# Order of 32 experts in a weight-streaming mixture-of-experts stage: number order with single blocks last, against heavy and light in turn

## The reference, cut to what matters

```
logits = x @ w_router + b_router
top_logit, top_idx = lax.top_k(logits, 4); gate = softmax(top_logit)
per expert e, over its tokens:
    h = x @ w_up[e] + b_up[e]              # 1024 -> 2048
    glu, lin = split(h); glu = min(glu, 7); lin = clip(lin, -7, 7)
    y = (glu * sigmoid(1.702 * glu) * (lin + 1)) @ w_down[e] + b_down[e]
    out[token] += gate * y
```

## Time and profile before

| | |
|---|---|
| runs shown | 1345.87 us median (1345.58 to 1346.92) |
| profiled execution, its time | 1348.95 us |
| profiled execution, its span | 1347.1 us |
| TensorE matmul busy | 1146.1 us, 85% of the span |
| DMA | 463.78 MB, mean 344 GB/s over the span |
| weight pieces | 192 of 2048 KB, 128 of `w_up` and 64 of `w_down` |
| mean granted TensorE clock | 0.93 of full speed |

### The profile page before, as it was taken

The page is one execution under the profiler, slowest core; times in us unless marked ns, Lnnn a source line. Parts: engine busy times, 40 slices in busy tenths (PEclk is TensorE's granted clock), DMA queues, the critical chain, the costliest instruction groups (busy, mean ns, idle before and its releaser), DMA issues.

```text
span 1347.1 us, 28518 instructions
## 1 busy us (share of the span) xinstructions
PE 1146.1 (85%) x10974; PEld 532.9 (40%) x10975; DVE 489.4 (36%) x1218; ACT 200.1 (15%) x297; POOL 224.7 (17%) x392
## 2 busy tenths in 40 slices
PE   6999999976999999999997987989889789964540
PEld 3445554543444444444543433424334334421120
DVE  2273453453334333333432332323333233321117
ACT  2114321011111111111211111111111111110001
POOL 1000012001222222222221211212122112210003
PEclk9999999986999999999998999989899889987775
DMA  9303005449699999979999999999999999999987
GB/s 341 117 1 125 16 1 221 154 175 406 268 421 414 415 417 423 426 293 426 426 427 426 426 424 427 426 427 424 424 425 419 423 428 425 426 427 426 424 328 302
DMA packets 51088, 463.78 MB, mean 344 GB/s; under 512 B 9052, under 2 KB 10264, under 8 KB 25976
## 3 DMA queue, kind: packets, MB, share of 16 engines
q1 hardware_dynamic: 41184, 441.89, 78.8%
q0 software_dynamic: 7632, 20.85, 4.0%
q10 hardware_dynamic: 2248, 0.71, 0.2%
HBM read 446.65 MB, written 16.78 MB: 344 GB/s over the span
## 4 chain that ended last, share of the span: by engine, by line
DMA 44%; PE 44%; SPq 4%; DVE 4%; issue 3%; ACT 0%; POOL 0%; ACTq 0%; POOLq 0%; DVEq 0%
DMA W<-in_w_up_dram 41%; PE B L1361 17%; PE B L1140 12%; PE B L1376 8%; PE B L1261 4%; SPq L305 1%; SPq L310 1%; DMA W<-yrow 1%; SPq L385 1%; SPq L387 1%; DMA yrow<-misc,idx_s 1%; DMA misc<-hsrow,idx_g 1%; DVE W L1112 0%; PE B L1284 0%; DMA W<-in_b_spatial_dram 0%
## 5 line engine op out<-in xcount | busy, mean ns | idle before, releaser
L1361 PE MATMUL B<-W,misc 128*32 128x512 f32 x4992 | 596.6, 626 | 124.4 <-DMA W<-in_w_up_dram 95.4
L1361 PEld LDWEIGHTS B<-W,misc 128*32 128x32 f32 x4992 | 188.1, 113 | 484.1 <-issue 474.8
L1376 PE MATMUL B<-W,misc 128*32 128x256 f32 x4992 | 289.0, 382 | 0.9 <-DVE misc L1053 0.9
L1376 PEld LDWEIGHTS B<-W,misc 128*32 128x32 f32 x4992 | 192.7, 111 | 120.3 <-issue 52.3
L1036 DVE TENSOR_TENSOR misc<-B,misc 128x512 f32<-128x512 f32 x78 | 54.0, 692 | 418.2 <-PE B L1361 418.2
L1140 PE MATMUL B<-W 128*128 128x512 f32 x384 | 171.2, 601 | 0.0
L671 ACT ACTIVATE misc<-misc 128x256 f32<-128x256 f32 x78 | 32.5, 416 | 850.4 <-DVE misc L1038 850.4
L502 POOL COPY idx_g<-idx_tab 128x1 uint32 (+1 forms) x79 | 15.0, 190 | 594.0 <-DVE misc L1067 576.7
L1140 PEld LDWEIGHTS B<-W 128*128 128x128 f32 x384 | 72.8, 194 | 85.6 <-issue 85.6
L514 POOL DMA_INDIRECT yrow<-misc,idx_s x78 | 78.4, 1006 | 160.0 <-DVE misc L1055 160.0
L671 ACT ACT_TABLE_LOAD x78 | 100.1, 1283 | 4.9 <-DVE idx_tab L1013 3.5
(11 more groups left out here) (257 smaller groups left out, 484.9 us busy)
## 6 DMA issues: line engine op xcount, KB each, us to landing
W<-in_w_up_dram SPq DMA_DIRECT2D x128, 2048.0 KB, 10.6
W<-in_w_down_dram SPq DMA_DIRECT2D x64, 2048.0 KB, 10.0
W<-in_w_in_dram SPq DMA_DIRECT2D x6, 2048.0 KB, 18.1
W<-yrow SPq DMA_DIRECT2D x4, 2048.0 KB, 14.5
W<-in_x_dram SPq DMA_DIRECT2D x8, 512.0 KB, 5.4
W<-in_w_out_dram SPq DMA_DIRECT2D x1, 4096.0 KB, 12.9
hres<-W SPq DMA_DIRECT2D x4, 512.0 KB, 2.6
hsrow<-W SPq DMA_DIRECT2D x4, 512.0 KB, 3.6
```

Source lines behind the costliest of these rows:

```text
L1361: ins = mm(B[0][BT * j:BT * (j + 1), :].rearrange("p (g h c) -> p g h c", g=2, h=2), xT[:, BT * k:BT * (k + 1)], up(par)[:, k, :, :, P * j ...
L1376: ins = mm(B[5][BT * j:BT * (j + 1), 0:QC], aT[:, BT * q:BT * (q + 1)], down(par)[:, q, QC * j:QC * (j + 1)], start=(q == 0), stop=(q == N ...
```

## The change

It replaces `late` by a weight for each expert: 32 times its blocks minus its number, and 4096 more for experts 0 and 1. `heavier` compares all pairs, a product with ones counts how many are heavier (the rank r), and `turn` gives the place: the smaller of 2r-1 and 62-2r, and for r = 31 64 more. A product with the identity lays `turn` out as a row, and `before` is where one turn is smaller than another. What follows in the kernel is as before.

With the block counts above the order becomes: experts 0 and 1, then a light and a heavy one in turn, the lightest with the heaviest first, the five-block expert in slot 3, and a single-block expert (25) last. In blocks: 3, 2, then 1, 5, 1, 4, 1, 4, 1, 4, then nine times 2, 3, and 2, 2, 2, 1.

```diff
-                    V.tensor_scalar(late[:, 1:2], partf[:, 0:1], 1.5, None, ALU.is_gt)
+                    link(V.tensor_scalar(late[:, 1:2], partf[:, 0:1], 1.5, 4096.0, ALU.is_lt, ALU.mult))
+                    V.tensor_tensor(late[:, 1:2], late[:, 1:2], partf[:, 0:1], ALU.subtract)
...
-            link(V.tensor_scalar(late[0:NE, 0:1], cnt[0:NE, 4:5], 1.0, late[0:NE, 1:2], ALU.is_equal, ALU.mult))
+            link(V.tensor_scalar(late[0:NE, 0:1], cnt[0:NE, 4:5], float(NE), late[0:NE, 1:2], ALU.mult, ALU.add))
...
             dve.wait_ge(s_late_e, 1)
-            link(V.scalar_tensor_tensor(before[0:NE, 0:NE], B[5][0:NE, 0:NE], late[0:NE, 0:1], tre[0:NE, 0:NE],
-                                        ALU.subtract, ALU.add))
-            V.tensor_scalar(before[0:NE, 0:NE], before[0:NE, 0:NE], 0.0, 1.0, ALU.max, ALU.min).then_inc(s_before, 1)
+            V.tensor_scalar(heavier[0:NE, 0:NE], B[5][0:NE, 0:NE], late[0:NE, 0:1], None, ALU.is_lt).then_inc(s_heavier, 1)
+            dve.wait_ge(s_rank, 1)
+            rank = B[5][0:NE, 64:65]
+            V.tensor_scalar(turn[0:NE, 0:1], rank, 2.0, -1.0, ALU.mult, ALU.add)
+            V.tensor_scalar(turn[0:NE, 1:2], rank, -2.0, 2.0 * NE - 2.0, ALU.mult, ALU.add)
+            link(V.tensor_scalar(turn[0:NE, 2:3], rank, NE - 1.5, 2.0 * NE, ALU.is_gt, ALU.mult))
+            link(V.scalar_tensor_tensor(turn[0:NE, 3:4], turn[0:NE, 0:1], turn[0:NE, 1:2], turn[0:NE, 2:3],
+                                        ALU.min, ALU.add))
+            V.tensor_scalar(turnb[0:NE, 0:NE], ones[0:NE, 0:NE], turn[0:NE, 3:4], None, ALU.mult).then_inc(s_turn, 1)
+            dve.wait_ge(s_turns, 1)
+            V.tensor_scalar(before[0:NE, 0:NE], B[5][0:NE, 128:128 + NE], turn[0:NE, 3:4], None, ALU.is_gt)\
+                .then_inc(s_before, 1)
...
             mm(B[5][0:NE, 0:NE], nbb[0:NE, P:P + NE], ident[0:NE, 0:NE], start=True, stop=True).then_inc(s_late_e, 1)
+            pe.wait_ge(s_heavier, 1)
+            mm(B[5][0:NE, 64:65], heavier[0:NE, 0:NE], ones[0:NE, 0:1], start=True, stop=True).then_inc(s_rank, 1)
+            pe.wait_ge(s_turn, 1)
+            mm(B[5][0:NE, 128:128 + NE], turnb[0:NE, 0:NE], ident[0:NE, 0:NE], start=True, stop=True).then_inc(s_turns, 1)
             pe.wait_ge(s_before, 1)
```

More of the change, by code:

```diff
@@ L210, in hybrid_layer @@
         late = r(4)
-        before = r(36)
+        before, heavier, turnb, turn = r(36), r(32), r(32), r(4)
         behind, atp = r(36), r(36)
@@ L268, in hybrid_layer @@
         s_w = [sems(f"s_w{par}_", 6) for par in range(2)]
+        s_heavier, s_rank, s_turn, s_turns = sem("s_heavier"), sem("s_rank"), sem("s_turn"), sem("s_turns")
         s_n2row, s_ytab = sem("s_n2row"), sem("s_ytab")
```

## The result

The changed kernel took 1336.09 us (median of 4 runs, 1334.56 to 1336.89), the kernel before beside it 1346.25 us: a ratio of 0.9923, 95% interval 0.9911 to 0.9935. That is 10.2 us faster. The forecast was 9.6 us faster and 1336.3 us. Two further sets of runs of the same kernel gave 0.9926 (0.9913 to 0.9940) and 0.9921 (0.9905 to 0.9936). The profiled execution of the changed kernel has a span of 1334.5 us.

The account below looks back on a forecast made before the run. The prediction took the weight stream as the bound, stopped for 13.1 us by TensorE's backlog; -13.1 + 2 (slot 3) + 1.5 (tables) = -9.6 us from 1345.87 gave 1336.3 us, range 1333.0 to 1342.5.

Parts of the forecast that it names:

- The bound, the mechanism: Expert stage: the weight stream bounds it; TensorE's backlog in slots 1 to 7 stops it; alternating order leaves no backlog.
- The removed backlog, -13.1 + 2 = -11.1 us: Stream from 367 to 610 us: the 13.1 us lost come back, less 2 us for slot 3.
- the 2 us at slot 3: End of the five-block slot: its buffer frees late, second piece 1.0 us too late; taken as 2, bounds 0 and 6.7.
- The table chain, +1.5 us: Table operations before the first gather: net +1.4 us, wholly on the path; taken as 1.5, bounds 1.0 and 2.5.
- The end, 0: After the last landing: last slot keeps one block, so nothing changes, between -1 and +1 us.
- The sum: Whole kernel: -13.1 + 2 + 1.5 = -9.6 us, giving 1336.3 us.
- The signs: Profile after: stream at 420 or more from 370 us, one dip at most, first up product about 1.5 us later.
- The loss only moves: Rival: front heavy slots stop the stream again, 10.5 us at slot 3, some at the next three; about 1345 us; chance 0.09.
- Half of it: Rival: 2.6 us of 367 to 550 not only backlog, slot 3 loses 5; 1341.9 us; chance 0.12.
- another order: Rival: table ranks come out otherwise than worked out, only the tables' 1.5 us sure; 1347.4 us; chance 0.05.
- Half clock in the heavy slots: Rival: second blocks of heavy slots run at 1.2 GHz, 17 us lost in place of 2; 1351.3 us; chance 0.08.
- 0.8 + 0.8 us: Heavy slot's first block behind a light slot: colder clock in last quarter and down product, counted within slot 3's 2 us.

Follow-up runs that it names:

- a_old_order: Changed kernel with its new table chain, but key and turn set to give the order of the kernel before; 1345.8 us, ratio 1.0001 to before.
- a_heavy_first: Changed kernel with the turn equal to the rank: heavy experts first, the five single blocks last; 1378.3 us, ratio 1.0233 to before.
- a_number: Changed kernel with experts in plain number order, single blocks where their numbers put them; 1364.2 us, ratio 1.0127 to before.
- b_bias_later: Changed kernel with SyncE's up bias load before the fourth piece, not the second, and down bias before the sixth, not the fifth; 1332.8 us, ratio 0.9907.
- b_three_ahead: Changed kernel with AHEAD = 3: a piece waits for the landing of the piece three before it; 1339.0 us, ratio 0.9947 to before.
- b_bias_later_old: Kernel before, with SyncE's two bias loads moved behind more of the weight pieces; 1344.1 us, ratio 0.9989 to before.
- d_before_again: Kernel before, unaltered, run again for a second profile; 1347.1 us, ratio 1.0002 to before.
- b_five_later: Changed kernel with the five-block expert ranked behind three three-block ones: slot 17, a four-block expert in slot 3; 1338.5 us, ratio 0.9940.

## Why the prediction was right, and where not

**The bound, the mechanism.** Right. The time is the stream's, the loss was the backlog of TensorE in slots 1 to 7, and the order took it away: shown by `a_old_order` (back with the old order), `a_heavy_first` (more of it) and `a_number` (gone with another order that strews the light ones).

**The removed backlog, -13.1 + 2 = -11.1 us.** Mis-sized: the stream got 8.2 us shorter (944.2 to 936.0 on average). One part of this is the 2 us at slot 3. I priced the second piece (1 us; measured 1.4) and missed the fifth, which waits for the output step of the last block, 1.3 us more: 2.7 in all, 0.7 above the term. `b_bias_later` shows both by removing them. The other part is larger: 2.2 us between 13.1 and 8.2 + 2.7 did not come back. In the profile of the changed kernel they lie in dips of under 1 us each, which the forecast held at nothing. One of them (1110 to 1120 us, with no wait of SyncE but for landings) did not come again, though the stream of that second profile was no shorter (936.2).

**The table chain, +1.5 us.** Right for the chain itself, 1.6 us; what it costs in the time is not settled. Four further passes cost 7.1 us, so nothing covers those. But the one pass that the change adds did not show with the old order (`a_old_order`, 1.0001). Part of it is won back right behind: from the first gather to the end of the first up product it takes 17.4 to 18.0 us in the three profiles with the old chain and 16.4 to 16.5 in the three of the changed kernel. These are the first up products, before and after:

```profile
320.41 9.30 PE L1361 MATMUL B<-W,misc 128*32 128x512 f32 x64 [3.74 <-DVE misc L1067]
```

```profile
318.77 8.77 PE L1376 MATMUL B<-W,misc 128*32 128x512 f32 x64 [2.36 <-DVE misc L1078]
```

Why that stretch is shorter no run shows, and in `a_old_order` it took 17.8 us.

**The end, 0.** Right within what can be read: from the last issue to the end of the span 54.6 to 57.3 us after, 54.9 and 56.7 before.

**The sum.** The terms as measured give -8.2 + 1.6 = -6.6 us, the runs -10.2. The missing 3.6 us were in no term of the forecast. In the profiles they lie ahead of the first piece of slot 2: the count's product starts some 3 us earlier in those of the changed kernel than in those of the kernel before, and about 1 us is won behind the first gather. Chance between executions does not explain them, since the three sets of the changed kernel, 15 runs, have medians within 0.6 us. The same sum (time against `before` of its set, less the change in the stream's length, less the chain) can be done for the other kernels of the table whose ends compare, all but `a_number` and `b_three_ahead`. The nine sets with the new chain come out 1.8 to 4.0 us faster than their terms, the two with the old chain (`b_bias_later_old`, `d_before_again`) about 0.5 us slower. So some 2 us or more go with the new code, in the old order too (2.5 us in `a_old_order`). The change adds one small VectorE operation ahead of the tables and removes none; the cause stays open. So the forecast came nearer than its terms deserve: an error of 2.9 us in the stream was covered by a gain that it did not foresee. That is luck.

**The signs.** No second block of a heavy slot ran over 7.1 us, SyncE waited 6.5 us for up products, TensorE waited for weights from slot 3 on (2.98 us at 402.84), and the last `w_down` piece was issued 10.7 us earlier. Two signs failed. There were two dips at slot 3 and a third place under 420 GB/s, and the first up product started 1.6 us earlier than before (318.77 against 320.41), not 1.5 later.

**The rivals.** "The loss only moves" fell: 2.7 us at slot 3, nothing at the three four-block slots. "Half of it" had 5 us at slot 3 and fell with it, and "another order" fell too, since the trace has the five blocks in slot 3. "Half clock in the heavy slots" fell, since no second block ran slow, but its smaller form is real. In slot 3 of the changed kernel the quarter behind the wait took 1.92 us in three profiles; in the same place of `b_three_ahead` and `b_five_later` it took 3.64, and in the first of these the fifth block came 3.1 us later and the stretch lost 6.0 us in place of 3.4. The forecast had 0.8 + 0.8 us for such a first block. The Trainium skill's rule in "TensorE: Matmul & The Clock Gate", section "HAM oscillation", that the group behind each such wait starts cold, agrees with the quarters of 3.64 us and not with those of 1.92.

## What to carry to other kernels

Where weights stream through two buffers, read the order of the work as a race between the stream and the engine. A run of heavy items builds a backlog that stops the stream at its end, light items at the tail leave it nothing to catch up, and heavy and light in turn remove the stop. Don't take the sum of the bubbles in such a stretch for the gain: 13.1 us of missing stream gave 8.2 here, and moving the bias loads gave 1.9 us of an expected 5 to 8 where TensorE bounded the stretch. List every wait of the issuing queue, small loads with waits of their own among them: here two bias loads between weight pieces cost 3.8 us, over a third of the order's gain. And compare the sum of the measured terms with the measured time, even when the forecast was met: here 3.6 us of the gain have no term.

## What the runs showed of the hardware

- A quarter of an up product that had waited about 3 us for its piece ran in 1.92 us or in 3.64 us in the same place of nearly the same kernel (402.84 in the changed kernel, 402.96 in `b_three_ahead`). The down product behind it then took 3.66 or 4.90 us.
- The stream ran at 425 GB/s with two pieces of 2 MB in flight, and with three at 426 (646 to 1094 us of `b_three_ahead`). At slot 3, where only one was left until the next issue at 447.86, it fell to 383 GB/s from 443 to 447 us and to 317 from 446 to 450 us.
- The start of the tables varied by 4.8 us between the fourteen profiles, half of the gain measured here.
